# Wider modulation products, and the first fourteen blocks of U taken in three rounded passes

## The reference

```python
def trunk_layer(x, cvec, l, mix, norm, peer, cache):
    sh1, sc1, gt1, sh2, sc2, gt2 = modulation(cvec, w_m, b_m)    # silu(cvec) @ w_mod + b_mod, 6144 wide
    h = x * (1.0 + sc1) + sh1
    y, new_state = even_mixer(...) or odd_mixer(...)
    x = layer_norm(DN_ALPHA * x + gt1 * y, g1, b1)
    h = x * (1.0 + sc2) + sh2
    x = layer_norm(DN_ALPHA * x + gt2 * peer_ffn(h, *peer), g2, b2)

def peer_ffn(h, w_q, sub_k1, sub_k2, u_tab, v_tab):
    q = (xt @ w_q)                       # scores against two sets of 128 keys, top 16 of each
    top_s, pos = lax.top_k(cand_s, 16)   # 16 of 16384 experts for each token and head
    g = softmax(top_s)
    act = gelu(einsum('chkd,cd->chk', u_tab[idx], x))
    return einsum('chk,chkd->cd', g * act, v_tab[idx])
```

## Time and profile before

| | us |
|---|---|
| median of three runs | 2478.13 |
| lowest and highest | 2476.19, 2481.86 |
| profiled execution | 2478.5 |
| its span (first to last instruction) | 2476.7 |
| PE busy | 2332.5 (94%) |
| DVE busy | 1760.7 (71%) |
| POOL busy | 907.1 (37%) |
| ACT busy | 758.4 (31%) |

### The profile page before, as it was taken

How to read it: one execution, slowest core, us unless ns; L and a number is a source line. 1 busy time by engine, 2 the same in 40 slices (tenths; PEclk the granted TensorE clock), 3 DMA queues, 4 the chain that set the end, 5 groups by cost and what they waited for, 6 DMA issues and landing times.

```text
span 2476.7 us, 33770 instructions
## 1 busy us (share of the span) xinstructions
PE 2332.5 (94%) x12534; PEld 1790.0 (72%) x12534; DVE 1760.7 (71%) x3593; ACT 758.4 (31%) x1366; POOL 907.1 (37%) x645
## 2 busy tenths in 40 slices
PE   4999799999999999999989688999999999999997
PEld 3756699789767867766667467987995777677664
DVE  2345479978668877777755446899784897777777
ACT  2354432123225422122243354311340452222221
POOL 3500460621211255555544115244113124555552
PEclk8999999999999999999989998999999999999999
DMA  7456334976899899999944812289669999999995
GB/s 276 139 209 231 107 111 133 396 288 209 284 332 327 322 391 383 380 388 393 357 142 135 243 38 84 90 286 403 200 203 357 329 332 341 393 379 379 401 377 209
DMA packets 219906, 679.69 MB, mean 274 GB/s; under 512 B 32384, under 2 KB 63152, under 8 KB 219232
## 3 DMA queue, kind: packets, MB, share of 16 engines
q1 hardware_dynamic: 143344, 398.00, 45.6%
q0 software_dynamic: 76400, 279.54, 29.9%
HBM read 658.87 MB, written 18.56 MB: 274 GB/s over the span
## 4 chain that ended last, share of the span: by engine, by line
PE 83%; DMA 7%; DVE 5%; ACT 2%; issue 1%; SPq 1%; POOL 1%; ACTq 0%
PE ps L1061 21%; PE ps L1038 15%; PE ps L734 12%; PE ps L735 12%; PE ps L736 12%; DMA ring<-in_u 4%; PE ps L1017 3%; PE ps L924 1%; PE ps L899 1%; PE ps L759 1%; DVE v_split L2049 1%; DMA ring<-in_w_mod 1%; PE ps L914 1%; PE ps L992 1%; DMA arena<-in_w_mod 1%
## 5 line engine op out<-in xcount | busy, mean ns | idle before, releaser
L658 POOL DMA_INDIRECT arena<-in_u_rows,arena x256 | 302.7, 1182 | 734.0 <-DVE arena L1865 553.6
L1061 PE MATMUL ps<-ring,arena 128*128 128x512 f32 x1264 | 564.2, 592 | 0.0
L658 POOL DMA_INDIRECT arena<-in_v,arena x256 | 356.2, 1391 | 321.1 <-DVE arena L1865 142.8
L1038 PE MATMUL ps<-arena,ring 128*128 128x256 f32 x2048 | 459.6, 382 | 11.5 <-DMA ring<-in_u 10.1
L1038 PEld LDWEIGHTS ps<-arena,ring 128*128 128x128 f32 x2048 | 384.0, 191 | 70.2 <-issue 18.3
L1061 PEld LDWEIGHTS ps<-ring,arena 128*128 128x128 f32 x1264 | 232.0, 190 | 243.8 <-issue 243.2
L1286 ACT ACTIVATE arena<-ps 128x256 f32<-128x256 f32 x256 | 98.2, 383 | 976.3 <-PE ps L736 612.4
L623 POOL TENSOR_TENSOR ring_lo<-ring,ring_hi 128x1024 fp32r<-128x1024 f32 x84 | 212.3, 2539 | 392.5 <-ACT ring_hi L1164 392.5
L734 PE MATMUL ps<-xs_high,u_split 128*128 128x256 f32 x1024 | 338.9, 331 | 0.0
L2078 DVE SCALAR_TENSOR_TENSOR arena<-arena 128x1024 f32<-128x1024 f32 x254 | 325.6, 1282 | 15.3 <-DVE arena L2078 0.5
L1865 DVE CUSTOM_DVE_ANT_0 arena<-arena 128x1024 f32<-128x1024 f32 x256 | 310.7, 1219 | 15.6 <-DMA arena<-in_u_rows,arena 14.3
(11 more groups left out here) (244 smaller groups left out, 3476.1 us busy)
## 6 DMA issues: line engine op xcount, KB each, us to landing
ring<-in_u SPq DMA_DIRECT2D x256, 512.0 KB, 6.5
ring<-in_v SPq DMA_DIRECT2D x256, 512.0 KB, 5.8
ring<-in_w_mod SPq DMA_DIRECT2D x80, 512.0 KB, 4.5
ring<-in_w_in SPq DMA_DIRECT2D x36, 512.0 KB, 3.3
ring<-in_w_q SPq DMA_DIRECT2D x32, 512.0 KB, 3.3
gelu_half<-arena SPq DMA_DIRECT2D x120, 128.0 KB, 4.9
arena<-gelu_half SPq DMA_DIRECT2D x120, 128.0 KB, 5.1
arena<-in_w_mod SPq DMA_DIRECT2D x16, 512.0 KB, 19.3
```

What stands on the lines that cost most here:

```text
L658: pool.indirect_dma_start(row[at], None, table, bass.IndirectOffsetOnAxis(where[:, k:k + 1], axis=0)).then_inc(sem(f"row_in{at}"), 16)
L1038: ins = mm(hidden_bank(b), slot[c % RING][:, P * k:P * k + P], HFS[:, k, :], start=(k == 0), stop=(k == KC - 1))
L1061: ins = mm(ps[:, t + 3 * q, :], GL[:, b % GLS, P * t - P:P * t], slot[c % RING][:, 512 * q:512 * q + 512], start=(b == MIDDLE[0]), stop=(b ...
```

## The change

Two things are changed. First, the modulation products take two chunks of w_mod at once: w_mod is laid out so that a chunk holds two pieces of 512 columns, and the four matmuls of a set have 512 columns and come from both chunks. PE waits for both chunks before the first of them, and frees the first slot with the second matmul and the second slot with the fourth. Second, the first 14 blocks of U of each layer are split: ACT's `high` for block b + 4 follows gelu(b), POOL's `low` for the blocks 4 to 13 stands before its gathers, and POOL also waits for PE's use of block 13. PICKED and PLAIN go from 37 and 39 to 39 and 41, so the 32 pieces of G are spread over 21 blocks (before: 23).

```diff
-PICKED = 37
-PLAIN = 39
+PICKED = 39
+PLAIN = 41
+SPLIT_FIRST = 14
...
-            raw.update(range(c0, c0 + 2 * KEYS))
+            raw.update(range(c0 + SPLIT_FIRST, c0 + 2 * KEYS))
...
             def experts(l):
                 c0 = start["uv", l]
+                split(c0 + RING, c0 + SPLIT_FIRST)
                 pool.wait_ge(sem("p_rows"), l + 1)
+                pool.wait_ge(used((c0 + SPLIT_FIRST - 1) % RING), turn_of(c0 + SPLIT_FIRST - 1))
...
-            def mod_products(g, n, w):
+            def mod_products(g, n, blocks_of, signals):
...
-                    at = LEAD + 32 * (4 * (n % 2) + j) - 2 * (g - first)
-                    r = slice(256 * (n // 2), 256 * (n // 2) + 256)
-                    ins = mm(ps[32 * j:32 * j + 32, 6 + batch % 2, r], cs[:, at:at + 32], w[:, 256 * j:256 * j + 256],
+                    at = LEAD + 32 * (4 * n + j) - 2 * (g - first)
+                    w = blocks_of[j // 2][:, 512 * (j % 2):512 * (j % 2) + 512]
+                    ins = mm(ps[32 * j:32 * j + 32, 6 + batch % 2, :], cs[:, at:at + 32], w,
...
+                    if j % 2 and signals:
+                        ins.then_inc(signals[j // 2], 1)
...
+                wait_loaded(pe, c + 1)
...
+                    if b < SPLIT_FIRST:
+                        columns_of(c, hidden_bank(b), P)
                         return
                     wait_loaded(pe, c)
...
                 for b in range(SPILL):
                     gelu(b)
+                    if b + RING < SPLIT_FIRST:
+                        high(u_chunk(l, b + RING))
```

More of the change, by code:

```diff
@@ L756, in mod_products @@
                 for j in range(4):
-                    at = LEAD + 32 * (4 * (n % 2) + j) - 2 * (g - first)
-                    r = slice(256 * (n // 2), 256 * (n // 2) + 256)
-                    ins = mm(ps[32 * j:32 * j + 32, 6 + batch % 2, r], cs[:, at:at + 32], w[:, 256 * j:256 * j + 256],
-                             start=(g == first and n == 0), stop=(g == first + groups - 1 and n == 3),
+                    at = LEAD + 32 * (4 * n + j) - 2 * (g - first)
+                    w = blocks_of[j // 2][:, 512 * (j % 2):512 * (j % 2) + 512]
+                    ins = mm(ps[32 * j:32 * j + 32, 6 + batch % 2, :], cs[:, at:at + 32], w,
+                             start=(g == first and n == 0), stop=(g == first + groups - 1 and n == 1),
                              skip_group_check=True)
+                    if j % 2 and signals:
+                        ins.then_inc(signals[j // 2], 1)
                 return ins
@@ L774, in _ @@
                 pe.wait_ge(sem(f"mod_in{g}"), 64)
-                for n in range(4):
-                    ins = mod_products(g, n, first_mod(4 * g + n))
+                for n in range(2):
+                    ins = mod_products(g, n, [first_mod(4 * g + 2 * n + i) for i in range(2)], None)
                 if g == MOD_FIRST - 1:
@@ L783, in _, with mod_chunks @@
             mod_columns(0)
-            def mod_chunk(stage, n):
-                g, q = MOD_STAGES[stage][0] + n // 4, n % 4
+            def mod_chunks(stage, n):
+                g, q = MOD_STAGES[stage][0] + n // 4, n % 4 // 2
                 c = start[stage] + n
                 wait_loaded(pe, c)
+                wait_loaded(pe, c + 1)
                 if q == 0 and g == BATCHES[BATCH_OF[g]][0]:
                     pe.wait_ge(sem("mod_ready"), BATCH_OF[g])
-                mod_products(g, q, slot[c % RING]).then_inc(used(c % RING), 1)
+                mod_products(g, q, [slot[(c + i) % RING] for i in range(2)], [used((c + i) % RING) for i in range(2)])
             def gate(n, c, q, bank):
@@ L927, in attention @@
                     if mods and n < PAIRS:
-                        mod_chunk(mods[0], mods[1] + 2 * n)
-                        mod_chunk(mods[0], mods[1] + 2 * n + 1)
+                        mod_chunks(mods[0], mods[1] + 2 * n)
                     if mods and mods[0] != "mod_b" and n == PAIRS + 1:
@@ L1035, in hidden @@
                         return
+                    if b < SPLIT_FIRST:
+                        columns_of(c, hidden_bank(b), P)
+                        return
                     wait_loaded(pe, c)
@@ L1099, in _ @@
                 if l == 0:
-                    for m in range(4):
-                        mod_chunk("mod_b", m)
+                    for m in range(0, 4, 2):
+                        mod_chunks("mod_b", m)
                 pe.wait_ge(sem("pr_evicted"), since("pr_evicted", l + 1))
@@ L1109, in _ @@
                 if l == 0:
-                    for m in range(28, 32):
-                        mod_chunk("mod_b", m)
+                    for m in range(28, 32, 2):
+                        mod_chunks("mod_b", m)
                     mod_columns(2)
@@ L2171, in wide @@
         return np.ascontiguousarray(w.transpose(3, 0, 2, 1, 4)).reshape(n // 128, 128, 1024)
-    def quarters(w):
-        w = w.reshape(2, 4, 128, w.shape[1] // 256, 256)
-        return np.ascontiguousarray(w.transpose(3, 0, 2, 1, 4)).reshape(-1, 128, 1024)
     odd = np.concatenate([np.arange(512).reshape(2, 4, 64).transpose(1, 0, 2).ravel(), np.arange(512, 2304)])
@@ L2215 @@
                           ).reshape(8, 8, 128).transpose(2, 0, 1).reshape(128, 64),
-        "w_mod": np.concatenate([quarters(g["w_mod"][l]) for l in range(2)]),
+        "w_mod": np.concatenate([wide(g["w_mod"][l]) for l in range(2)]),
         "w_in0": wide(np.roll(np.pad(g["ev_w_in"][0], ((0, 0), (0, 96))), 512, axis=1)), "w_in1": wide(g["od_w_in"][0][:, odd]),
```

## The result

The changed kernel took 2461.18 us (median of five runs, 2459.48 to 2466.55), the kernel before 2478.13 beside it. The ratio is 0.9935, with a 95% interval of 0.9921 to 0.9949: 16 us faster, between 13 and 20. Forecast were 2466.5, that is a ratio of 0.9953, inside the stated range and just outside the interval: the sign was right and the size 5 us too small.

The account below looks back on a forecast made before the run. PE bounds U before the gathers, transfers set the pace beside them. Passes -16.4, DVE and POOL +1.4, pieces +1.9, pairs +1.5 make -11.6 from 2478.5: 2466.9 profiled, 2466.5 against the median; range 2458 to 2478.

Parts of the forecast that it names:

- Three passes: First 14 blocks of U on PE: 2.87 us each instead of 3.45, saving 8.2 us a layer.
- The split keeps up: First 14 blocks of U: ACT's 1.06 us and POOL's 2.54 a block stay under PE's 2.87.
- the loop over two blocks: Split U blocks: load landing, ACT's copy, a gelu and two issues take 5.6 us, just hidden behind PE's 5.7.
- the slow chain: Rival at ACT's copy in the split blocks: waits for loads hold PE, losing 3.5 us a layer, 2489.9; chance 0.08.
- The stretch with gathers keeps the lead: U blocks beside the gathers: PE enters 2.4 blocks ahead and stays so, with the picks near 528 us.
- The rival that it is absorbed: Stretch with gathers: PE's lead of 2.4 blocks is lost waiting at the loads, giving 2479.6 us; chance 0.07.
- DVE and POOL: First top 16 beside POOL's low parts: DVE 7.8 us late, PE's block 13 late by 0.7 a layer, 1.4 in all.
- Pieces of G: 32 pieces in 21 blocks instead of 23: only the last is late, about 0.9 us a layer, 1.9 in all.
- Modulation pairs: Modulation products, two chunks at once: no gain on PE, waiting for both chunks costs 1.5 us in all.
- the later release of the first slot: Layer 1's first attention: first product behind the wait and slot freed later, delaying the next load; 1.1 us by its end.

Follow-up runs that it names:

- store_first: Whole change, but for the split blocks SP issues the store of block b ahead of the load of b + 4: 2510.27 us (one run; before 2480.68).
- exp8: Whole change, with the exponentials of the prompt's scores after gelu(8) instead of gelu(10): 2471.41 us (one run).
- pieces23: Whole change with the old PICKED and PLAIN, 37 and 39, so the pieces of G lie in 23 blocks: ratio 0.9928 (0.9912 to 0.9945).
- mod_only: Kernel before with only the modulation products taken in pairs of chunks, U unchanged (37 and 39): ratio 0.999 (0.998 to 1.0).
- null_before: Kernel before, unchanged, profiled once more: ratio 0.9997 (0.9984 to 1.001).
- dots34_18: Whole change with 38 and 40, four dots moved behind the first one-hots, 18 split blocks instead of 14: ratio 0.9951 (0.9935 to 0.9968).
- dots34_16: Whole change with 38 and 40, four dots moved behind the first one-hots, 16 split blocks instead of 14: ratio 0.9944 (0.9922 to 0.9966).
- dots34_14: Whole change with 38 and 40, four dots moved behind the first one-hots, 14 split blocks kept: ratio 0.9933 (0.9917 to 0.995).

## Why the prediction was right or wrong

**Three passes** (8.2 a layer): right. From the start of the first to the start of the fifteenth, 14 blocks took 40.39 us where 14 float32 blocks took 48.35, 7.96 less; the first block is 0.07 longer than the others.

**The split keeps up**: right, and for the reason given. Landing 3.7, the loop over two blocks covered; store_first shows what it is when it isn't. One of the signs was ill chosen: waits of ACT's copies above 1 us a block were to show the slow chain, and ACT did wait 1.3 us ahead of nine copies, but PE did not.

**The stretch with gathers keeps the lead**: right. Behind it, PE started block 39 at 136.6 us from the end of the scores (526.50 less 389.89); before, it was 144.5 (picks at 529.33 in the earlier trace rows, and two blocks): the 7.9 is still there. Over the five executions of the table it is 8.3 on average. The rival that it is absorbed is out.

**DVE and POOL** (0.7 a layer, the step that failed most clearly): the mechanism is right and the size was not. DVE's operations are held to the end of a low part, each by up to 2.2 us, but two of five in layer 0 and one of five in layer 1 of the changed kernel, and the top 16 came 4.5 late in layer 0, not 7.8. The five were not all that could be held: in layer 1 a copy of 0.17 us behind them took 1.65. POOL was not back to back: between 404 and 419 it waited 0.2 to 0.7 us for ACT's copy ahead of four of six low parts, and short operations went through there. ACT would have begun to stand at 5.9 late (423.75 against 417.9), and PE only at some 7 late: in exp8 the block that waits starts 2.1 us behind the end of the top 16, and here block 13 was due at 427.2. So the price was 0 and not 1.4 in all. (By its own terms the sum gives 430.2 for gelu(11), not 430.4.) How many of the five would meet a low part was a guess in the prediction. The page "SBUF — State Buffer" of the Trainium skill, section "Who interferes with whom", has the rule by which the held operations wait for the whole of POOL's instruction; the 2.45 and 2.80 us agree with it.

**Pieces of G** (0.9 a layer): right at the last piece. The lead of 8.3 at block 39 is 7.5 at the end of the stage, on average: 0.8 lost. What I did not see is that with 23 blocks a stall (1.13 in layer 0, 0.73 in layer 1 of pieces23) comes at the first piece, so that against the old numbers 21 blocks cost nothing: pieces23 has the same U stages.

**Modulation pairs** (1.5): the gain of zero was right, the cost was not there. In mod_only the waits for w_mod in the ring came to 9.6 us, in the kernel before to 10.2, in null_before to 9.0. The time of mod_only, 0.999 (0.998 to 1.0), does not reach the 1.0006 that 1.5 us would be. Why the later release of the first slot did not add up, as I had reckoned, was not tried.

In sum: forecast were -16.4 (passes) + 1.4 (DVE and POOL) + 1.9 (pieces) + 1.5 (pairs) = -11.6. By the stages of five profiled executions it is -16.6 (the lead of 8.3 at block 39, twice), 0, +1.6 and 0, that is -15.0. The interval of the measured ratio, 13 to 20 us, holds that. The first and the third term were right; the other two were waits that the sum priced and that cost nothing, one because it had slack, the other for a reason that is open. The measured time lies within the range because the passes are by far the largest term; the three costs together were 4.8 in the forecast and 1.6 in the stages.

## What to carry to other kernels

A price read from the same operation elsewhere in the trace (2.87 for a block in three passes) held to 0.01 us. Of three waits walked one held (the last piece) and two cost nothing; of the one with DVE and POOL the lateness was 7.8 in the forecast and 4.5 in the trace, as the gaps of the other engine had been underrated. Ask for every forecast stall from which lateness on it begins to cost, and read that slack from the engine that waits, before its size is estimated. And where a stage gets shorter on one engine, look for the next engine in its chain: here DVE's work ahead of the one-hots took back what blocks 15 to 18 could give.

## What the runs showed that was not expected

In exp8 PE waited 3.10 us, and the granted clock, 1.00 (2.4 GHz) ahead of the wait, was 0.62 on average over the 4.4 us behind it. Some eight records ran at full speed first, then the clock was 0.50 (1.2 GHz) from 426.8 to 429.9, with records 0.41 us long in place of 0.28; the block behind the wait took 1.6 us more. In dots34_18 it fell too, behind PE's wait of 2.72 at the picks:

```profile
522.90:526.20 3.30, 3.30 (x12) 2.92 (x13) 3.30 (x7) 1.25 (x3) 0.00 (x0) 0.54 0.84 330
```

Behind the waits of 0.4 us ahead of the blocks beside the gathers it did not fall: the clock there is 1.00. In exp8 the price of the stall was half as much again as the stall.

The first 140 us, up to the attention scores, took 139.3 us in store_first and 143.5 in dots34_16, which do the same there, and layer 1's first attention 108.2 in the change and 112.0 in dots34_14; a gain of 1 us in a stage of 256 is visible in the stage's own landmarks and not in the time of the whole.
